# A differential attention head's two softmaxes subtracted before the product by the values

## The reference

```
o[h, a] = softmax(mask(q[h, a] @ k[h, a].T / 8)) @ v[h]          a = 0, 1
o[h]    = o[h, 0] - lam * o[h, 1]
o_b     = rms_norm(o) * subln * (1 - lambda_init)
```

## Time and profile before

| | |
|---|---|
| median of 3 runs | 1121.16 us (1121.11 to 1121.27) |
| span of the profiled execution, first to last instruction | 1118.7 us |
| TensorE busy (matmuls) | 1076.4 us, 96% |
| VectorE busy | 334.3 us, 30% |
| ScalarE busy | 196.4 us, 18% |
| GpSimd busy | 36.6 us, 3% |
| DMA | 438.65 MB, mean 392 GB/s |
| chain that ended last | TensorE 75%, DMA 20%, VectorE 3%, ScalarE 1%, issue 1% |

### The profile page before, as it was taken

How to read it: one execution, slowest core, us unless ns; L and a number is a source line. 1 busy time by engine, 2 the same in 40 slices (tenths; PEclk the granted TensorE clock), 3 DMA queues, 4 the chain that set the end, 5 groups by cost and what they waited for, 6 DMA issues and landing times.

```text
span 1118.7 us, 12699 instructions
## 1 busy us (share of the span) xinstructions
PE 1076.4 (96%) x5198; PEld 506.6 (45%) x5198; DVE 334.3 (30%) x611; ACT 196.4 (18%) x338; POOL 36.6 (3%) x45
## 2 busy tenths in 40 slices
PE   9999999999999999999999898989898989898998
PEld 8888878734343343434343333324242424242432
DVE  4887767313121221212122112112121203021212
ACT  7676675500000000100010000000000000000000
POOL 1007120000000000000000000000000000000000
PEclk9999999999999999999999999999999999999999
DMA  9763349999999999999999999999999999999997
GB/s 363 293 202 137 128 139 425 380 416 427 427 428 428 428 428 426 434 431 431 431 431 432 431 432 432 432 432 431 431 432 431 432 431 432 432 431 431 425 425 294
DMA packets 27843, 438.65 MB, mean 392 GB/s; under 512 B 3232, under 2 KB 3488, under 8 KB 6560
## 3 DMA queue, kind: packets, MB, share of 16 engines
q1 hardware_dynamic: 26928, 431.46, 91.5%
q10 hardware_dynamic: 880, 6.69, 1.5%
HBM read 437.08 MB, written 1.05 MB: 392 GB/s over the span
## 4 chain that ended last, share of the span: by engine, by line
PE 75%; DMA 20%; DVE 3%; ACT 1%; issue 1%; POOL 0%; SPq 0%; POOLq 0%; ACTq 0%; DVEq 0%
PE bank L927 25%; PE bank L953 20%; DMA ring<-in_expert_q 20%; PE bank L499 11%; PE bank L895 6%; PE bank L858 5%; PE bank L486 3%; PE bank L777 2%; DVE ring_s L1424 1%; PE bank L550 1%; PE bank L599 0%; DVE gate_r L1455 0%; PE bank L893 0%; PE bank L624 0%; PE bank L587 0%
## 5 line engine op out<-in xcount | busy, mean ns | idle before, releaser
L927 PE MATMUL bank<-ring,feat_r 128*64 128x512 f32 x1504 | 337.6, 602 | 13.4 <-DMA ring<-in_expert_q 13.4
L927 PEld LDWEIGHTS bank<-ring,feat_r 128*64 128x64 f32 x1504 | 105.3, 138 | 235.5 <-issue 211.8
L953 PE MATMUL bank<-ring,feat_r 128*64 128x512 f32 x768 | 173.2, 596 | 7.9 <-DMA ring<-in_expert_q 7.4
L1711 DVE TENSOR_SCALAR late_r<-bank 128x512 f32<-128x512 f32 x32 | 22.1, 692 | 426.7 <-PE bank L927 426.7
L499 PE MATMUL bank<-ring_s,feat_s 128*128 128x512 f32 (+2 forms) x428 | 129.7, 384 | 0.2 <-issue 0.2
L927 PE MATMUL bank<-pool_r,feat_r 128*64 128x512 f32 x512 | 118.5, 610 | 10.6 <-DMA pool_r<-in_expert_q 10.5
L953 PEld LDWEIGHTS bank<-ring,feat_r 128*64 128x64 f32 x768 | 54.0, 137 | 113.8 <-issue 109.8
L1321 ACT ACTIVATE late_r<-late_r 128x512 f32<-128x512 f32 x32 | 20.2, 630 | 469.1 <-DVE late_r L1711 469.1
L1735 DVE TENSOR_TENSOR acc_r<-bank,acc_r 128x512 f32<-128x512 f32 x64 | 44.3, 691 | 151.2 <-PE bank L895 151.2
L499 PEld LDWEIGHTS bank<-ring_s,feat_s 128*128 128x128 f32 x428 | 76.6, 188 | 13.2 <-issue 1.5
L499 PE MATMUL bank<-ring_s 128*128 128x512 f32 (+2 forms) x212 | 79.7, 376 | 0.0
(11 more groups left out here) (215 smaller groups left out, 673.5 us busy)
## 6 DMA issues: line engine op xcount, KB each, us to landing
ring<-in_expert_q SPq DMA_DIRECT2D x45, 4096.0 KB, 27.4
ring<-in_expert_q SPq DMA_DIRECT2D x41, 2048.0 KB, 19.1
pool_r<-in_expert_q SPq DMA_DIRECT2D x15, 4096.0 KB, 29.1
pool_r<-in_expert_q SPq DMA_DIRECT2D x16, 2048.0 KB, 19.0
ring<-in_head_w SPq DMA_DIRECT2D x23, 1024.0 KB, 4.8
ring<-in_expert_q SPq DMA_DIRECT2D x21, 1024.0 KB, 13.4
ring<-in_head_w SPq DMA_DIRECT2D x6, 768.0 KB, 10.6
qkT_r<-in_expert_q ACTq DMA_DIRECT2D x1, 2048.0 KB, 12.5
```

Source lines behind the costliest of these rows:

```text
L927: mm = pe.matmul(b[e * SLOTS:(e + 1) * SLOTS, :], xT[:, k, e * SLOTS:(e + 1) * SLOTS], w[:, e, g, :], start=(late and k == 0), stop=(k == ...
L953: mm = pe.matmul(bank[4 + h][e * SLOTS:(e + 1) * SLOTS, :], aT[k // 4][:, k % 4, e * SLOTS:(e + 1) * SLOTS], w[:, q, e, :], start=(k == 0) ...
L1711: ts(glu, bank[2 * f][:], LIMIT, None, ALU.min).then_inc(sem(f"glu_ready{f}"), 1)
```

## The change

Ahead of the product, VectorE now forms one matrix of weights for each differential head. With e0, e1 the two subheads' exponentials and s0, s1 their row sums, `combine(i)` computes `e0 - lam * (s0 / s1) * e1` in place of e0 (columns of m = 0 and m = 1 apart, as their rows have different sums); one turn and one product by the values follow, and `diff_out(i)` multiplies by 1/s0 straight into `o_b`. Four turns and four products go, and so do four of the eight outputs, `o_raw` and the difference over all heads.

The exponentials are taken in place: `scored` has the four slots that `scored` and `probs` had together, and mask s waits for the turn that read slot s-4. The order of the differential stage is written out anew on TensorE, ScalarE and VectorE: both subheads of a head follow each other closely in masks and exponentials. The reciprocals for GpSimd and `lam` are taken at the stage's start. The MLA stage keeps its order. Five pairs of semaphores are merged into one each, and waits counted by subheads are counted by turns (t = 0..3 for the heads, 4..11 for the MLA heads). The core of the diff:

```diff
-        o_raw = latT_r.rearrange("p (m h d) -> p m h d", m=NM, h=SUB)
...
-        scored, probs, probsT = soft[:, 0:2], soft[:, 2:4], soft[:, 4:6]
+        scored, probsT = soft[:, 0:4], soft[:, 4:6]
...
+        def weights_at(t):
+            return (2 * t if t < HD else t + HD) % 4
...
                 elif s_ == 0:
-                    sp.wait_ge(sem("ob_diffed"), NM)
-                    sp.wait_ge(sem("valued"), SUB + HA)
+                    sp.wait_ge(sem("valued"), HD + HA)
...
-            def probs_turn(s):
-                if s == 0:
+            def probs_turn(t):
+                if t == 0:
                     pe.wait_ge(sem("unit_copied"), 2 * 14)
-                pe.wait_ge(sem("exped"), 2 * (s + 1))
-                if s >= 2:
-                    pe.wait_ge(sem("probsT_copied"), s - 1)
+                if t < HD:
+                    pe.wait_ge(sem("combined"), NM * (t + 1))
+                else:
+                    pe.wait_ge(sem("exped"), 2 * (t + HD + 1))
+                if t >= 2:
+                    pe.wait_ge(sem("probsT_copied"), t - 1)
                 for i in range(3):
-                    mm = turn(bank[2 + s % 2][:, i * P:(i + 1) * P], probs[:, s % 2, i * P:(i + 1) * P])
+                    mm = turn(bank[2 + t % 2][:, i * P:(i + 1) * P], scored[:, weights_at(t), i * P:(i + 1) * P])
                 mm.then_inc(sem("probs_turned"), 1)
 
-            def values(s):
-                pe.wait_ge(sem("probsT_copied"), s + 1)
-                if s >= 2:
-                    pe.wait_ge(sem("headed"), s - 1)
-                n = DV if s < SUB else VA
-                b = bank[4 + s % 2]
+            def values(t):
+                pe.wait_ge(sem("probsT_copied"), t + 1)
+                if t >= 2:
+                    pe.wait_ge(sem("headed"), t - 1)
+                n = DV if t < HD else VA
+                b = bank[4 + t % 2]
...
                 def v_of(m):
-                    return dv[:, m, (s // 2) * DV:(s // 2 + 1) * DV] if s < SUB else va[:, m, s - SUB, :]
-
-                pT = probsT[:, s % 2]
+                    return dv[:, m, t * DV:(t + 1) * DV] if t < HD else va[:, m, t - HD, :]
+
+                pT = probsT[:, t % 2]
...
-            def step(s, first, last):
-
-                if s < last:
-                    if s >= SUB:
-                        scores(s)
-                    elif s > 0 and s % 2 == 0:
-                        diff_scores(s // 2)
-                    if s == SUB:
-                        for half in range(2):
-                            pe.wait_ge(sem(f"qkaT_copied{half}"), HA // 2)
-                    if s == HEADS - 1:
-                        o_b_turn(0)
-                    if s != SUB - 1:
-                        gate_part(s, 0)
-                if s > first:
-                    probs_turn(s - 1)
-                if s == SUB - 1:
-                    gate_part(s, 0)
-                elif s < last:
-                    gate_part(s, 1)
-                elif s == SUB:
-                    gate_part(s - 1, 1)
-                if s > first:
-                    values(s - 1)
-
-
             n0 = chunk_index("w_in", 0, O_DV)
             split_part(unit(13), n0, range(KD // 2))
             pe.wait_ge(sem("unit_copied"), 2 * 13)
             diff_scores(0)
             split_part(unit(13), n0 + 1, range(KD // 2, KD))
-            for s in range(SUB + 1):
-                step(s, 0, SUB)
+            gate_part(0, 0)
+            gate_part(0, 1)
+            diff_scores(1)
+            gate_part(1, 0)
+            probs_turn(0)
+            gate_part(1, 1)
+            values(0)
+            gate_part(2, 0)
+            gate_part(2, 1)
+            gate_part(3, 0)
+            probs_turn(1)
+            gate_part(3, 1)
+            values(1)
+            diff_scores(2)
+            gate_part(4, 0)
+            gate_part(4, 1)
+            diff_scores(3)
+            gate_part(5, 0)
+            gate_part(5, 1)
+            probs_turn(2)
+            gate_part(6, 0)
+            values(2)
+            gate_part(6, 1)
+            gate_part(7, 0)
+            probs_turn(3)
+            gate_part(7, 1)
+            values(3)
 
             pe.wait_ge(sem("qka_ready"), 2 * NM)
             pe.wait_ge(sem("scored"), SUB)
-            pe.wait_ge(sem("probsT_copied"), SUB)
             for p_, i in enumerate(QKA_ORDER):
                 if p_ in (4, 5):
-                    pe.wait_ge(sem("headed"), SUB - 5 + p_)
+                    pe.wait_ge(sem("headed"), HD - 5 + p_)
...
-            act.wait_ge(sem("lambda_summed"), 1)
-            act.activation(lam[:, 2:4], lam[:, 0:2], ACT.Exp).then_inc(sem("lambda_exped"), 1)
+            act.wait_ge(sem("lambda_steps"), 1)
+            act.activation(lam[:, 2:4], lam[:, 0:2], ACT.Exp).then_inc(sem("lambda_steps"), 1)
...
             def exps(s):
                 act.wait_ge(sem("maxed"), 2 * (s + 1))
-                if s >= 2:
-                    act.wait_ge(sem("probs_turned"), s - 1)
                 for m in range(NM):
                     c = slice(0, P) if m == 0 else slice(P, 3 * P)
-                    act.activation(probs[:, s % 2, c], scored[:, s % 2, c], ACT.Exp, bias=nmax[:, 2 * s + m:2 * s + m + 1],
+                    act.activation(scored[:, s % 4, c], scored[:, s % 4, c], ACT.Exp, bias=nmax[:, 2 * s + m:2 * s + m + 1],
...
-            def probsT_copy(s):
-                act.wait_ge(sem("probs_turned"), s + 1)
...
+            def probsT_copy(t):
+                act.wait_ge(sem("probs_turned"), t + 1)
+                if t >= 2:
+                    act.wait_ge(sem("valued"), t - 1)
+                act.copy(probsT[:, t % 2], bank[2 + t % 2][:, 0:3 * P]).then_inc(sem("probsT_copied"), 1)
+
+            def gates_copy(g):
+                act.wait_ge(ring_used, chunk_index("w_in", 4, O_GATE + g * HALF) + 1)
+                for m in range(NM):
+                    act.activation(gates[:, m, g * HALF:(g + 1) * HALF], bank[6 + m][:], ACT.Copy,
+                                   scale=rstd[:, m:m + 1]).then_inc(sem("gates_copied"), 1)
+
+            act.wait_ge(sem("lat_ready"), 4)
+            exps(0)
+            exps(1)
+            act.wait_ge(ring_used, chunk_index("w_in", 4, O_DV) + 1)
+            for m in range(NM):
+                project_copy(13, m, dv[:, m], WD)
+            split_hi(14)
+            probsT_copy(0)
+            exps(2)
+            exps(3)
+            split_hi(15)
+            probsT_copy(1)
+            gates_copy(0)
+            split_hi(16)
+            exps(4)
+            exps(5)
+            exps(6)
+            probsT_copy(2)
+            exps(7)
+            split_hi(17)
+            probsT_copy(3)
+            gates_copy(1)
...
             def scale_mask(s):
                 dve.wait_ge(sem("scores"), s + 1)
-                if s >= 2:
-                    dve.wait_ge(sem("exped"), 2 * (s - 1))
+                if s >= 4:
+                    before_t = (s - 4) // 2 if s - 4 < SUB else s - 4 - HD
+                    dve.wait_ge(sem("probs_turned"), before_t + 1)
...
-                stt(scored[:, s % 2], bank[s % 2][:, 0:3 * P], scale, mask, ALU.mult, ALU.add).then_inc(sem("scored"), 1)
+                stt(scored[:, s % 4], bank[s % 2][:, 0:3 * P], scale, mask, ALU.mult, ALU.add).then_inc(sem("scored"), 1)
...
+            def combine(i):
+
+                s = 2 * i
+                one, two = scored[:, s % 4], scored[:, (s + 1) % 4]
+                r, by = rsum[:, 2 * s:2 * s + 4], rsum[:, 2 * s + 2:2 * s + 4]
+                dve.wait_ge(sem("exped"), 2 * (s + 2))
+                link(dve.reciprocal(r, sums[:, 2 * s:2 * s + 4]))
+                link(stt(by, sums[:, 2 * s:2 * s + 2], lam[:, 5:6], by, ALU.mult, ALU.mult))
+                for m in range(NM):
+                    c = slice(0, P) if m == 0 else slice(P, 3 * P)
+                    stt(one[:, c], two[:, c], by[:, m:m + 1], one[:, c], ALU.mult, ALU.add).then_inc(sem("combined"), 1)
+
+            def diff_out(i):
+
+                dve.wait_ge(sem("valued"), i + 1)
+                if i == 0:
+                    dve.wait_ge(sem("qkd_turned"), NM)
+                tt(o_b[:, :, i, :], v3(bank[4 + i % 2][:, 0:2 * DV], 2),
+                   rsum[:, 4 * i:4 * i + 2].unsqueeze(2).broadcast_to([P, NM, DV]), ALU.mult).then_inc(sem("headed"), 1)
...
             def head_out(s):
                 dve.wait_ge(sem("exped"), 2 * (s + 1))
                 link(dve.reciprocal(rsum[:, 2 * s:2 * s + 2], sums[:, 2 * s:2 * s + 2]))
-                dve.wait_ge(sem("valued"), s + 1)
-                n = DV if s < SUB else VA
-                dst = o_raw[:, :, s, :] if s < SUB else o_a[:, :, s - SUB, :]
-                tt(dst, v3(bank[4 + s % 2][:, 0:2 * n], 2), rsum[:, 2 * s:2 * s + 2].unsqueeze(2).broadcast_to([P, NM, n]),
-                   ALU.mult).then_inc(sem("headed"), 1)
+                dve.wait_ge(sem("valued"), s - HD + 1)
```

(123 more changed lines are left out.)

68 lines of the change are left out of this document (9 added, 59 removed).

## The result

The changed kernel takes 1126.9 us (median of 5 runs, 1126.39 to 1127.1) against 1121.16: the ratio is 1.0047, with a 95% interval of 1.0037 to 1.0058. It is 5.7 us slower, where the forecast was 5.1 us faster; the profiled execution took 1126.97.

What follows compares the result with a forecast made beforehand. TensorE's instructions bound the differential stage, the expert weight stream the end. Removed turns (1.44) and products (2.80) make 4.24 us, the new order 0.9 more: 5.12 off 1121.16 gives 1116.1 us, range 1115.0 to 1118.6.

Steps and rivals of the forecast that it cites:

- TensorE's sum: Differential stage: four turns and four products removed (4.24 us) plus the new order save 5.12 us on TensorE.
- a microsecond in the stage is one at the end: Expert weight stream starts after the differential stage, so each microsecond saved there counts in full at the end.
- VectorE's prices: VectorE's list in the differential stage: a combine 1.2 us, a split 1.49, a masked score 1.13, a lambda link 0.18.
- The granted clock: TensorE in the differential stage: granted clock stays at 1.00, the upper level of 2.4 GHz.
- So the added VectorE work costs nothing, covered by TensorE's gate parts: Ahead of the four head turns: each combine is ready before TensorE comes, with slacks of 1.7, 1.4, 1.6, 1.9 us.
- the bound of 2.4: Upper bound in us for one combine: its four instructions each at a 512-wide one's price, less their overlap.
- the rows show a stretch of 0.60 of VectorE's instruction at most, and none of GpSimd's: Differential stage: reading of how far VectorE and GpSimd disturb each other, a split taking up to 1.78 us against 1.18 alone.
- both halves took equally long (13.56 and 13.59): GpSimd's two halves in the old profile, six splits beside it: taken as evidence against its being held up by VectorE.
- The rule of the Trainium skill: VectorE instructions with two SBUF inputs and GpSimd ones reading SBUF exclude each other for the whole instruction, whoever comes first.
- rival (b): GpSimd held up by VectorE's two-input instructions, MLA turns wait: net 9.2 us slower, 1130.3 us; chance 0.04.
- rival (a): VectorE sets the pace at the turns, a combine costing 2.4 us: 2.2 saved, 1118.9 us; chance 0.11 with similar waits.
- Rival (c): Stream of expert weights ends when it did despite the faster stage: 1121.2 us; chance 0.05.

Runs made afterwards that it cites:

- the two kernels with GpSimd idle: Changed kernel and kernel before, each with GpSimd's norm and rotation of the MLA heads left out: 1115.87 and 1121.23 us.
- the PSUM version: Changed kernel with combine's small instructions on scalar operands and each head's second subhead's exponentials in PSUM: 1117.91 us, measured again 1117.17.
- the two new orders: Combines 0 and 1 ahead of splits 13 and 14: on the PSUM version 1120.91 us; with only the small instructions on scalar operands 1124.22 us.

## Why the prediction was wrong

**Right.** TensorE's sum held: 5.12 us in the prediction, 5.4 between the two kernels with GpSimd idle; the MLA turns were forecast at 116.94 and came at 117.20 there, in a trace that stands 0.20 later, and 1116.1 us were forecast, 1115.87 measured there. That a microsecond in the stage is one at the end held in both directions. VectorE's prices held wherever GpSimd was idle: combine 1.14 (1.2 taken). ScalarE cost nothing.

**Wrong beside the main step.** The granted clock, forecast to stay at 1.00, was 0.89 in the stage, behind waits of TensorE that the prediction did not have.

**The step that failed** is "So the added VectorE work costs nothing, covered by TensorE's gate parts", and in it the price of a combine beside GpSimd: "1.2 us in all with the stretch beside GpSimd", with the bound of 2.4, and "the rows show a stretch of 0.60 of VectorE's instruction at most, and none of GpSimd's". Combine 0 took 3.5 us (93.21 to 96.70) and combine 1 4.2 (104.59 to 108.79), lambda 1.77 where 0.18 was taken, splits 2.75 and 3.75 where 1.49 was. Slacks of 1.7 and 1.4 us became waits of 3.36 and 3.69. The split's 1.49 was a mean over six meetings each of which began shortly before a GpSimd instruction ended. The first of them, in the trace of the kernel before, was

```profile
91.62 1.55 DVE L1377 TENSOR_TENSOR ring_s<-ring,ring_s 128x1024 fp32r<-128x1024 f32 x1 [1.32 <-ACT ring_s L1029]
```

and the GpSimd instruction that began at 89.32 and took 2.76 ended at 92.08, 0.46 after it was issued. The stretch was read as a rate, a factor on VectorE's time that grows with the work. It is a wait, up to a whole GpSimd instruction (0.7 to 2.8 us), and does not depend on the size: it fell on an instruction over one column.

The second half was misread from a merged row. GpSimd's two instructions of line 314 stood as one row:

```profile
92.16 4.49 POOL L314 TENSOR_TENSOR pool_r<-pool_r,rows_sb 128x768 f32<-128x768 f32 x2
```

Taken apart in the trace of the kernel before, they are

```profile
92.16 2.69 POOL L314 TENSOR_TENSOR pool_r<-pool_r,rows_sb 128x768 f32<-128x768 f32 x1
```

```profile
94.81 1.84 POOL L314 TENSOR_TENSOR pool_r<-pool_r,rows_sb 128x768 f32<-128x768 f32 x1
```

the same work, 2.69 with a split in its way and 1.84 without. That both halves took equally long (13.56 and 13.59) only meant that each was held up as often. The rule of the Trainium skill, SBUF — State Buffer, section Who interferes with whom, was quoted and set aside; all traces here agree with it, the one before the change too, as its six splits show. It was priced on one side only: GpSimd being held by VectorE, which is rival (b) with its chance of 0.04. What decided was the other side, VectorE held by GpSimd, for which the prediction had no price but the stretch of its row. It came in the shape of rival (a), TensorE waiting for VectorE, but not by (a)'s sum: (a) took 2.4 us for a combine and let four of them eat every slack, while two of 3.5 and 4.2, with dearer splits ahead of them, made waits of 7.0 us at turns 0 and 1 and none at turns 2 and 3, where GpSimd was done. Rival (b) did show, mildly: GpSimd ran 27.7 us instead of 27.15 in the changed kernel, and in the PSUM version 31.2, late by 0.8.

Rival (c) fell: the stream follows the stage one to one. Of the 10.7 us lost at the MLA turns 3.2 are longer matmuls behind the waits, at the lowered clock, of which 0.6 came back when the clock alone was held up.

## What to carry to other kernels

Where GpSimd works for long in SBUF, count VectorE's instructions with two SBUF inputs on the critical path, tiny ones too, and price each at a wait of up to one GpSimd instruction; then try one input from PSUM, or scalar operands, before a new order. Here the first gave 4.2 us against the kernel before, and the two new orders gave none. A stretch seen in a trace beside another engine is not a rate: look at the single instructions' starts and ends on both engines. An order of instructions may owe microseconds to where such meetings fall, so a shift of a small instruction needs a measurement of its own.

## What the runs showed of the hardware

- VectorE and GpSimd took turns by whole instructions when VectorE's had two SBUF inputs: a one-element subtraction took 1.77 us instead of 0.15, 74 splits ended 1.08 to 1.09 us behind the end of the GpSimd instruction that they met, and GpSimd's 1536 columns took 3.72 instead of 2.76 when a split came 0.05 us before it.
- With one of the two inputs in PSUM, or with scalar operands for the second, the same arithmetic did not wait in any of these traces: 0.74 for both large instructions, 0.20 for the small one.
- Behind idle times of 3.4 and 3.7 us TensorE's granted clock was 0.70 and 0.53, partly its lower level (1.2 GHz), and its matmuls lost 3.2 us; with the clock held at 1.00 by idle turns the stage was only 0.6 us shorter, as VectorE still set the pace at turn 1.
